# GpSimd builds the first one-hot block of every other batch of the second dense tile

## The reference, cut to what matters

```
x = x + peer(rmsnorm(x), w_q, keys1, keys2, u_tab, v_tab)

def peer_block(xb):                      # 128 tokens, D = 2048
    ...                                  # 8 heads, 16 of 128*128 = 16384 experts each
    e = i1 * 128 + i2                    # expert numbers, (128 tokens, 8 heads, 16)
    g = softmax(sv)
    act = gelu(einsum('thkd,td->thk', u_tab[e], xb))
    return einsum('thk,thkd->td', g * act, v_tab[e])
```

## Time and profile before

| | |
|---|---|
| three runs | 3857.77, 3867.67, 3869.97 us |
| the profiled execution's own time | 3870.63 us |
| its span (first to last instruction) | 3868.8 us |
| mean granted TensorE clock | 0.895 of full speed |
| busy: PE, DVE, ACT, POOL | 3051.7, 2591.0, 586.0, 1394.5 us |
| build of the second dense tile in the trace | about 2800 to 2866 us |

### The profile page before, as it was taken

One profiled execution on the slowest core, in us unless ns is written; L12 is line 12 of the kernel. 1 busy time (PEld: TensorE's weight loads), 2 busy tenths in 40 slices (PEclk: granted clock), 3 DMA queues, 4 the chain that ended last, 5 costly groups with the idle time before them and its releaser, 6 DMA issues.

```text
span 3868.8 us, 34526 instructions
## 1 busy us (share of the span) xinstructions
PE 3051.7 (79%) x11870; PEld 1937.8 (50%) x11870; DVE 2591.0 (67%) x3611; ACT 586.0 (15%) x1115; POOL 1394.5 (36%) x876
## 2 busy tenths in 40 slices
PE   6999989987999989888345544544179899999993
PEld 6999989975555545555112212222143334444441
DVE  2788830035777766666688887889985556665658
ACT  4444320010010000111100001222250000000000
POOL 2000000003343333324476667666612234434344
PEclk9999999989999999999676677777599999999996
DMA  4222367759899998889899999999849999999998
GB/s 125 85 84 85 97 188 241 238 191 353 327 383 391 369 380 333 321 339 355 339 410 405 407 401 404 357 383 378 316 182 350 365 408 418 421 421 421 421 422 357
DMA packets 394596, 1244.91 MB, mean 322 GB/s; under 512 B 22785, under 2 KB 268289, under 8 KB 268959
## 3 DMA queue, kind: packets, MB, share of 16 engines
q0 software_dynamic: 120720, 876.60, 56.4%
q1 hardware_dynamic: 258944, 356.03, 26.4%
q10 hardware_dynamic: 14815, 10.87, 0.9%
HBM read 1232.26 MB, written 12.00 MB: 322 GB/s over the span
## 4 chain that ended last, share of the span: by engine, by line
DMA 35%; PE 27%; DVE 20%; issue 10%; POOL 5%; ACT 1%; SPq 1%; DVEq 0%; POOLq 0%; ACTq 0%
DMA region<-in_v_tab_dram,region 26%; PE ps L1588 14%; DVE region L1418 6%; DMA region<-in_u_tab_dram,region 5%; POOL region L607 5%; DVE region L1366 4%; PE ps L1571 3%; PE ps L1573 3%; PE ps L1572 3%; DVE region L1357 1%; DMA region<-in_w_q_dram 1%; DMA region<-scores_kept 1%; DVE region L1315 1%; DVE region L1312 1%; DMA region<-in_w_in_dram 1%
## 5 line engine op out<-in xcount | busy, mean ns | idle before, releaser
L607 POOL DMA_INDIRECT region<-in_u_tab_dram,region x544 | 886.8, 1630 | 1488.5 <-DVE region L1357 578.8
L1588 PE MATMUL ps<-region,region 128*128 128x160 f32 (+1 forms) x5120 | 1208.7, 399 | 67.3 <-DMA region<-in_w_out_dram 20.1
L1588 PEld LDWEIGHTS ps<-region,region 128*128 128x128 f32 x5120 | 852.2, 194 | 415.5 <-issue 43.1
L1418 DVE SCALAR_TENSOR_TENSOR region<-region,region 128x2048 f32<-128x2048 f32 x384 | 869.5, 2287 | 105.0 <-DMA region<-in_u_tab_dram,region 104.3
L1818 PE MATMUL ps<-region,region 128*128 128x512 f32 x2048 | 890.4, 597 | 38.8 <-DMA region<-in_v_tab_dram 38.0
L1366 DVE SCALAR_TENSOR_TENSOR region<-region,region,region 128x2048 f32<-128x2048 f32 x224 | 526.8, 2352 | 560.5 <-DMA region<-in_v_tab_dram,region 548.9
L1818 PEld LDWEIGHTS ps<-region,region 128*128 128x128 f32 x2048 | 389.7, 191 | 538.9 <-issue 483.2
L607 POOL DMA_INDIRECT region<-in_v_tab_dram,region x288 | 469.5, 1630 | 423.8 <-DVE region L1366 338.6
L1766 PE MATMUL ps<-region,region 128*128 128x512 f32 x512 | 355.8, 861 | 330.3 <-DMA region<-in_v_tab_dram,region 305.7
L1766 PEld LDWEIGHTS ps<-region,region 128*128 128x128 f32 x512 | 139.2, 285 | 532.2 <-issue 505.9
L1357 DVE SCALAR_TENSOR_TENSOR region<-region,region 128x2048 f32<-128x2048 f32 x160 | 363.0, 2286 | 17.7 <-DMA region<-in_u_tab_dram,region 17.6
(11 more groups left out here) (227 smaller groups left out, 1681.0 us busy)
## 6 DMA issues: line engine op xcount, KB each, us to landing
region<-in_v_tab_dram SPq DMA_DIRECT2D x128, 1024.0 KB
region<-in_w_in_dram SPq DMA_DIRECT2D x192, 512.0 KB
region<-in_w_out_dram SPq DMA_DIRECT2D x64, 512.0 KB
region<-in_w_q_dram SPq DMA_DIRECT2D x64, 512.0 KB
region<-in_w_a_dram SPq DMA_DIRECT2D x32, 512.0 KB
region<-in_w_b_dram SPq DMA_DIRECT2D x32, 512.0 KB
region<-in_u_tab_dram,region POOLq DMA_INDIRECT x544, 12.0
region<-in_x_prompt_dram SPq DMA_DIRECT2D x7, 1024.0 KB, 16.1
```

Source lines behind the costliest of these rows:

```text
L607: pool.indirect_dma_start(out=slot, out_offset=None, in_=rows_ap, in_offset=bass.IndirectOffsetOnAxis(ap=idx[:, k:k + 1], axis=0)).then_in ...
L1418: stt(out=u_b[s], in0=u_b[s], scalar=1.0, in1=xn_tile(UNITS_A + u), op0=ALU.mult, op1=ALU.mult, accum_out=dots[u % 2][:, k:k + 1]).then_in ...
L1588: last = mm(outs[n][:, 0:WIDTH[g]], wide[s][:, q, n * P:(n + 1) * P], rhs(k), start=(k == 0), stop=(k == n_k - 1))
```

## The change

POOL makes the first one-hot block of the odd batches of the second dense tile; DVE makes the first block of the even ones, and the second block of these, as before. The eight instructions of two neighbouring batches are thus split four and four. POOL does batches 1 to 15 just ahead of its gather z = 7, batches 17 to 23 ahead of z = 8 and 25 to 31 ahead of z = 9 (`POOL_AT`). It waits, as DVE did, for `turn_read` and for `built`, and raises a semaphore of its own. PE waits for `pool_ones` in the odd batches and counts `a_ones` anew in the even ones.

```
+def on_pool(t, b):
+    return t == 1 and b % 2 == 1
...
+POOL_AT = [7 + max(0, b // 8 - 1) for b in range(BATCHES)]
...
+        pool_ones = sem("pool_ones")
...
+            def first_ones(b):
+                n = BATCHES + b
+                pool.wait_ge(turn_read, 2)
+                pool.wait_ge(built, n - 1)
+                for q in range(BATCH):
+                    col = BATCH * b + q
+                    last = nc.gpsimd.tensor_scalar(one_a[n % 2][:, q, :], count, turned[:, 0, col:col + 1],
+                                                   turned[:, 2, col:col + 1], ALU.is_equal, ALU.mult)
+                last.then_inc(pool_ones, 1)
+
             for z in range(P + V_LAG + 1):
+                for b in range(BATCHES):
+                    if on_pool(1, b) and POOL_AT[b] == z:
+                        first_ones(b)
...
                 if on_dve(t, b):
                     tt(one_b[n % 2], count.unsqueeze(1).to_broadcast([P, BATCH, P]),
                        turned[:, 1, BATCH * b:BATCH * (b + 1)].unsqueeze(2).to_broadcast([P, BATCH, P]), ALU.is_equal)
+                if on_pool(t, b):
+                    return
                 for q in range(BATCH):
...
-                pe.wait_ge(a_ones, n + 1)
+                if on_pool(t, b):
+                    pe.wait_ge(pool_ones, b // 2 + 1)
+                else:
+                    pe.wait_ge(a_ones, n + 1 if t == 0 else BATCHES + b // 2 + 1)
```

## The result

The changed kernel took 3893.72 us (median of 6 runs, 3887.10 to 3899.48), the kernel before 3866.11 us beside it: ratio 1.0072, 95% interval 1.0054 to 1.0090. In a second comparison it was 3899.85 against 3862.38 us, 1.0102 (1.0083 to 1.0122). So by the ratios it is slower by 28 us (21 to 35) and 39 us (32 to 47), where 3 us, no change to be measured, was forecast.

The account below looks back on a forecast made before the run. The build of the second dense tile, paced by ACT and PE, was taken as the bound; 0 (undisturbed pairs) + 2.8 (dots) + 0.4 (start) = +3.2 us gave 3871 us, range 3860 to 3892.

Parts of the forecast that it names:

- What bounds the kernel: Build of the second dense tile, paced by ACT and PE at 3.84 us a pair; a microsecond there is one at the end.
- The deadline: POOL's odd block may start when the previous odd batch is built, and PE wants it 2.67 us later.
- The price of POOL's instruction: Each POOL block instruction was taken at 0.40 us; four a set, so undisturbed pairs cost nothing but have no cover left.
- My own sum: POOL's set in an undisturbed pair: 0.25 + 4 x 0.40 + 0.60 + 0.26 = 2.7 us, against 2.67 allowed.
- the second rival: POOL bounds the build: 0.70 us an instruction, 1.2 us late a pair, +18 to +28 us, 3886 to 3896; chance 0.29.
- Getting in each other's way: POOL waits for DVE's instruction to end, then gets its turn; alternating with DVE's short ones adds 0.60 + 0.26 us.
- my net + 2.8: At three dots in the build: 2.7 us POOL delay plus 2.4 us lowered PE clock, less 2.3 us saved.
- The last batch: Build's end: gather z = 9 goes out behind batch 31's block, before the last batch is built; put at nothing.
- DVE's earlier start on the dots: DVE, not waiting for the odd batch, starts each dot some 2 us earlier, removing PE's wait: at most 2.3 us saved.
- The start: First batch of the build: two POOL instructions in between delay it by up to 0.8 us, partly hidden: +0.4 us.
- The gathers moved behind POOL's blocks: POOL's gathers z = 7, 8 and 9 now stand behind its blocks; nothing queued waits longer, put at nothing.
- The first rival: POOL keeps pace everywhere at 0.3 us an instruction; every pair but the first runs at 3.84: -2.3 us, 3865; chance 0.18.

Follow-up runs that it names:

- 8 and 12 sets: Changed kernel with only 8 or 12 odd batches' first blocks on POOL, none beside a dot: ratios 1.0031 and 1.0049 against the kernel before.
- batch 31 alone: Changed kernel with only the first block of batch 31 on POOL, DVE making the others: build 75.7 us, ratio 1.0014 against the kernel before.
- the run aside: DVE makes all first blocks as in the kernel before; POOL repeats the odd batches' into an unread spare tile: build 65.4 us, ratio 1.0039.
- the run with half sets: Changed kernel with POOL making only tokens 2 and 3 of each odd batch, DVE 0 and 1: build 77.7 us, ratio 1.0027 against the kernel before.

## Why the prediction was wrong, point by point

**What bounds the kernel: right.** A microsecond of build is about one of the whole (8 and 12 sets; for batch 31 alone the whole shows less, 5 of 10, within its interval). That DVE stood in ACT's shade holds: with the second blocks moved from ACT to DVE the build isn't longer.

**The deadline: right.** 2.67 us; two instructions kept it, four at 0.82 us didn't.

**The price of POOL's instruction: the step that failed.** I took 0.40 us, from the select's 288 ns and the rate of a two-input operation, between ends of 0.29 and 0.86. It is 0.81 with DVE quiet, near the end that I had called high. The nearest row in shape wasn't the nearest in price: the comparison in a `tensor_scalar` costs 0.54 us by itself, nearly twice the select. A set is 3.30 us, so every pair is late, + 15.8 us for the eleven undisturbed pairs where I had put nothing. With PE at full clock a pair is 0.92 us late, and the deadline gives just that: 0.14 until POOL starts, 3.30, 0.14 until PE starts, less 2.67, is 0.91. My own sum with 0.82 us would have been 1.7 late; two of its terms were too large, the 0.25 for POOL's start and the 0.86 for DVE's short instructions, which cost nothing in these pairs. In six of the eleven PE ran at half clock, which is another 0.92 each. My forecast had no such term there; the second rival had.

By the Trainium skill, "GPSIMD Engine Reference", section "Performance pitfalls for Q7 kernels", an estimate of mine had been 0.17 us for two small reads; the two per-partition operands cost 0.81 - 0.65 = 0.16 us. That estimate was good, what it was added to was not.

**Getting in each other's way: right that POOL waits for a long instruction of DVE's, too low in size.** I had 0.9 us for each dot; the set is 2.5 us longer, and with the price the three pairs are + 10.7 us in place of my net + 2.8. With short instructions on DVE the sum of 0.86 us was too much: 0 to 0.4 us.

**The last batch: forgotten, the second step that failed.** I counted three dots between the groups, and not that DVE, freed of batch 31, goes straight on to the dots that follow, and that POOL's last set then lies under a row of them: + 9.7 us, a quarter of the loss. I had called DVE's earlier start on the dots a gain. From the gathers' spacing I had also taken it that POOL gets a turn between two dots; its first `tensor_scalar` got none between three.

**The start: + 0.4 forecast, + 0.5 measured, but that is luck.** I expected DVE's first batch to be delayed; PE began it 1.87 us behind the first squares, 1.86 before. The half microsecond stands at the odd batch, for which PE waited until POOL's set of 3.35 us was done. **The gathers moved behind POOL's blocks:** put at nothing, and the changed kernel shows nothing; but the run aside, 15 us slower, suggests what it costs once POOL is late and the build isn't.

**The rivals.** The second one, POOL as the bound at 0.70 us, had the mechanism and 3886 to 3896 us; I gave it 0.29. That its number fits is in part luck: it had + 18 to + 28 us from the pairs, where the undisturbed pairs gave 15.8 and the dots and the last set another 20. The range ended at 3892, just below the median. The first rival is out with the price, the last one (gathers freed earlier) did not come about, as POOL was late. The dots placed inside the build show that there is something in it: 9 us.

## What to carry to other kernels

Work moved to an idle engine has a deadline, not a share of busy time: read from the loop when the input is there and when the output is wanted, and measure the very form of the instruction alone before it is moved, as another operation of the same shape can cost half. Then look at what the engine that was freed does next: here it went on to long instructions that held up the one that had taken its work. And where an engine has a pause inside a loop that another one bounds, see whether it can do work on which later transfers wait: here that was worth 9 us.

## What the runs showed of the hardware

- On POOL, a `tensor_scalar` of 128x128 in fp32 took 0.54 us for a comparison with a constant, 0.61 with a per-partition operand, 0.65 for comparison and multiplication with constants, 0.81 with two such operands. Addition and multiplication with two operands took 0.45 us, less than a multiplication alone with one operand (0.60 us); why, stays open.
- A POOL `tensor_scalar` that meets a DVE dot (two inputs, 2.29 us) waits for it to end: one dot made a set of four 2.5 us longer. In a row of dots it gets no turn at the first two gaps: one instruction took 7.13 us, under three dots, in the changed kernel, 7.12 with batch 31 alone on POOL and 6.87 in the run with half sets. Why, stays open; a gather got a turn with every dot. By the Trainium skill, "SBUF — State Buffer", section "Who interferes with whom", an operation with two SBUF inputs contends with a GpSimd one that reads SBUF; that POOL waits at the dots agrees.
- DVE lost little from the other side: its `tensor_tensor` of 0.69 us was 0.87 us long beside POOL, and the build wasn't longer by it.
- PE's granted clock was 0.67 in the changed build and 0.90 before. A pair took 5.67 us at half clock and 4.75 at full. Keeping PE busy raised the mean to 0.82 and gained nothing, as DVE then met POOL's sets earlier.
